# State recurrence of an S5 layer: a third chain on GpSimd, and conditioning loads issued by the sync engine

## What is computed

```
bu = einsum('blgh,gph->blgp', u, bb)             # input to the states
s_t = a * s_(t-1) + bu_t                         # complex, diagonal; scan over the positions
y = einsum('blgp,ghp->blgh', s_re, c_re) - einsum('blgp,ghp->blgh', s_im, c_im)
z = gelu(d*u + y_forward + y_backward) @ w_glu
```

## Time and profile before

| | us |
|---|---|
| median of 3 runs | 3016.66 |
| lowest and highest run | 3013.38, 3018.93 |
| the profiled execution | 3012.23 |
| its span from first to last instruction | 3010.4 |
| recurrence on VectorE, first to last start | 1856.9 to 1948.4 |
| its 124 products, 128 x 256 elements, mean | 0.412 |
| its 248 sums, 128 x 128 elements, mean | 0.279 |

### The profile page before, as it was taken

The page is one execution under the profiler, slowest core; times in us unless marked ns, Lnnn a source line. Parts: engine busy times, 40 slices in busy tenths (PEclk is TensorE's granted clock), DMA queues, the critical chain, the costliest instruction groups (busy, mean ns, idle before and its releaser), DMA issues.

```text
span 3010.4 us, 42044 instructions
## 1 busy us (share of the span) xinstructions
PE 2663.3 (88%) x16522; PEld 2155.4 (72%) x16522; DVE 1925.7 (64%) x1959; ACT 1073.1 (36%) x856; POOL 112.0 (4%) x169
## 2 busy tenths in 40 slices
PE   6969999986368899999999985759979999999997
PEld 3438888722357788888888873258868888888886
DVE  7866666544955677676777763846676666655554
ACT  3333333323313333333443423023433333344442
POOL 1020000000000100000000002110001000000000
PEclk9989999988678999999999997979989999999999
DMA  8988888544004388787887859667837777555551
GB/s 246 351 275 269 277 268 275 170 127 152 0 0 154 113 279 279 258 285 267 281 276 261 284 175 210 182 172 258 289 134 235 234 241 235 192 193 185 181 182 55
DMA packets 289270, 639.64 MB, mean 212 GB/s; under 512 B 76371, under 2 KB 79317, under 8 KB 285589
## 3 DMA queue, kind: packets, MB, share of 16 engines
q1 hardware_dynamic: 243844, 601.22, 60.6%
q0 software_dynamic: 6400, 19.21, 2.2%
q10 hardware_dynamic: 38928, 17.86, 2.2%
HBM read 614.24 MB, written 19.79 MB: 211 GB/s over the span
## 4 chain that ended last, share of the span: by engine, by line
PE 76%; DVE 12%; DMA 4%; ACT 3%; ACTq 3%; issue 2%; SPq 1%; DVEq 0%
PE PS L267 45%; PE PS L268 23%; DMA araw<-in_ada_w 2%; ACTq L972 2%; ACT Pb L928 2%; DVE Pb L1639 2%; DVE acc L1634 1%; PE PS L873 1%; PE PS L449 1%; PE PS L714 1%; PE PS L220 1%; PE PS L735 1%; PE PS L184 1%; DMA omat<-WF 1%; DVE HF L1567 1%
## 5 line engine op out<-in xcount | busy, mean ns | idle before, releaser
L267 PE MATMUL PS<-H,whi 128*128 128x512 f32 x5888 | 2077.8, 398 | 98.7 <-DVE wlo L257 75.3
L268 PE MATMUL PS<-H,wlo 128*128 128x256 f32 x5888 | 1653.3, 281 | 0.0
L267 PEld LDWEIGHTS PS<-H,whi 128*128 128x128 f32 x5888 | 1112.9, 189 | 366.7 <-DVE wlo L257 81.4
L257 DVE TENSOR_TENSOR wlo<-raw,whi 128x2048 fp32r<-128x2048 f32 x368 | 843.1, 2292 | 734.0 <-ACT whi L253 733.1
L253 ACT ACTIVATE whi<-raw 128x2048 fp32r<-128x2048 f32 x368 | 705.5, 1918 | 1252.9 <-PE PS L268 1219.4
L268 PEld LDWEIGHTS PS<-H,wlo 128*128 128x128 f32 x5888 | 1118.7, 190 | 0.0
L176 DVE SCALAR_TENSOR_TENSOR acc<-araw,cact,acc 128x1024 f32<-128x1024 f32 x240 | 307.0, 1279 | 0.7 <-DMA araw<-in_ada_w 0.3
L928 ACT ACTIVATE Pb<-PS 128x1024 f32 (+5 forms) x117 | 118.3, 1035 | 180.9 <-issue 69.3
L928 ACT ACTIVATE H<-Pb 128x512 fp32r (+2 forms) x142 | 94.9, 669 | 42.2 <-DVE Pb L1338 28.3
L1745 POOL TENSOR_SCALAR X<-X,small 128x256 f32<-128x256 f32 x64 | 54.7, 867 | 1084.0 <-DVE Pb L1338 1083.9
L1386 DVE TENSOR_TENSOR H<-Pb,H 128x512 fp32r<-128x512 f32 x128 | 87.5, 684 | 0.0
(11 more groups left out here) (251 smaller groups left out, 1446.6 us busy)
## 6 DMA issues: line engine op xcount, KB each, us to landing
raw<-in_mlp_w SPq DMA_DIRECT2D x256, 1024.0 KB, 6.1
araw<-in_ada_w SPq DMA_DIRECT2D x308, 512.0 KB, 4.4
raw<-in_mix_w_in SPq DMA_DIRECT2D x64, 1024.0 KB, 7.7
raw<-in_s_w_glu SPq DMA_DIRECT2D x32, 1024.0 KB, 7.4
acc<-in_ada_w SPq DMA_DIRECT2D x44, 512.0 KB, 6.9
raw<-in_mix_w_out SPq DMA_DIRECT2D x16, 1024.0 KB, 5.1
vmat<-Pb ACTq DMA_DIRECT2D x8, 1024.0 KB, 7.6
omat<-WF ACTq DMA_DIRECT2D x16, 512.0 KB, 13.2
```

What stands on the lines that cost most here:

```text
L257: nc.vector.tensor_tensor(wlo[:, s % 2, :], raw[:, s, :], whi[:, s % 2, :].bitcast(F), ALU.subtract).then_inc(S("lo_done"), 1)
L267: nc.tensor.matmul(PS[:, b, :], w[0], H2[:, :, k, :], start=first, stop=False, skip_group_check=True)
L268: return nc.tensor.matmul(PS[:, b, 0:T], w[1], H2[:, 0, k, :], start=False, stop=last, skip_group_check=True)
```

## The change

VectorE keeps 96 of the 128 groups, as two chains of 48 with a semaphore each. The other 32 groups go to GpSimd as a third chain, with its own semaphore and its own products in `acc[:, 512:640]`. The instructions are the same on both engines and are written once, in `recurrence`. GpSimd starts its chain when all increments are copied and the first state is zeroed. TensorE waits for both engines before `across`. The 32 loads of the shift parts leave GpSimd's queue, and SP issues them, with the same waits, between the inner matrices and the last four output matrices.

```diff
-    STP = acc[:, 0:512].rearrange("p (h a c x) -> p h a c x", h=2, a=2, c=2)
+    STP = acc[:, 0:384].rearrange("p (h a c x) -> p h a c x", h=2, a=2, c=2)
+    STP_POOL = acc[:, 512:640].rearrange("p (h a c x) -> p h a c x", h=1, a=2, c=2)
+
+    def recurrence(engine, q, chains, products):
+        A4v = A4[:].rearrange("p (a c) x -> p a c x", a=2)
+        done = 0
+        for k in range(2, 64):
+            for h, (steps, xs) in enumerate(chains):
+                if k > 2:
+                    q.wait_ge(S(steps), done)
+                old = SV[:, k - 1, :, xs].unsqueeze(1).broadcast_to([P, 2, 2, xs.stop - xs.start])
+                engine.tensor_tensor(products[:, h], A4v[:, :, :, xs], old, ALU.mult).then_inc(S(steps), 1)
+            for a_ in range(2):
+                for h, (steps, xs) in enumerate(chains):
+                    q.wait_ge(S(steps), done + 1 + a_)
+                    new = SV[:, k, :, xs]
+                    engine.tensor_tensor(new, new, products[:, h, 1, ::-1] if a_ else products[:, h, 0], ALU.add
+                                         ).then_inc(S(steps), 1)
+            done += 3
+        for steps, _ in chains:
+            q.wait_ge(S(steps), done)
...
@@ sync, after the loads of IM
+                    sp.wait_ge(S(f"{GATE2.name}_freed"), 1)
+                    for c in range(32):
+                        if c < 4:
+                            sp.wait_ge(S("ada_used"), SCALE3.base + PRIME_ADA)
+                        else:
+                            sp.wait_ge(S("shift_used"), c - 3)
+                        row, col = (3 * KT + c // 2) * P, (c % 2) * ADA_HALF
+                        sp.dma_start(SHB[c % 4], ada_w[row:row + P, col:col + ADA_HALF]
+                                     ).then_inc(S(f"sh_ready{c % 4}"), 16)
...
@@ tensor
-                pe.wait_ge(S("s5_scan"), 1)
+                pe.wait_ge(S("s5_scan"), 2)
...
@@ vector: the loop over k with its two halves is replaced by
+                    recurrence(nc.vector, v, (("scan_steps", slice(0, 48)), ("scan_other", slice(48, 96))), STP)
                     v.sem_inc(S("s5_scan"), 1)
...
@@ gpsimd: the loop of 32 loads is replaced by
+            pool.wait_ge(S("sv_evac"), 8)
+            pool.wait_ge(S("win_ready"), 3)
+            recurrence(nc.gpsimd, pool, (("pool_steps", slice(96, 128)),), STP_POOL)
+            pool.sem_inc(S("s5_scan"), 1)
```

## The result

Over 20 runs of each, the changed kernel has a median of 3022.8 us against 3010.73 us: ratio 1.0034, with a 95% interval of 1.0018 to 1.0050, some 5 to 15 us. The forecast was slower, by 68 us.

What follows compares the result with a forecast made beforehand. VectorE's recurrence in layer 1 was taken to set the end, TensorE waiting 9.6 us. VectorE's 75 us plus GpSimd's 85 us against 91.9 gave +68 us on 3012.2, 3080, set at 3082 us; range 3015 to 3105.

Steps and rivals of the forecast that it cites:

- The sign: Whole kernel: the change makes it slower, by 68 us in the likeliest case; chance of slower 0.81.
- the order, one chain after the other: Layer 1's recurrence: GpSimd stands still until VectorE's chains end, so 75 + 85 = 160 us against 91.9; chance 0.53.
- The rival by turns: Recurrence: GpSimd gets in after each VectorE instruction, costing VectorE 0.52 us a step; +15 to +30 us, 3027 to 3047; chance 0.27.
- VectorE alone: Recurrence: VectorE's 96 groups need 1.21 us a step, 75.1 us for 62 steps.
- GpSimd alone: Recurrence: GpSimd's product and two sums need 1.37 us a step, 85 us in all, bounds 74 and 91.
- Serial order: Recurrence: VectorE's chains, then GpSimd's, take 160 us together, from 1856.9 to 2017.
- The clock behind the scan: TensorE after the recurrence: a longer wait costs next to nothing more in clock, 27 products a us against 28.
- The loads: Conditioning loads moved to SP: first lands near 1885, TensorE ready at 1948 to 1956, hidden behind the scan; uncovered -1 to +7 us.
- The 9.6 us as the most to be had: TensorE's wait before line 873: the most a shorter recurrence can give with everything else left alone.

Runs made afterwards that it cites:

- the experiment on kinds: Changed kernel with GpSimd's chain replaced by chained MEMSETs, TENSOR_SCALARs, COPYs and sums, 32 of 128 groups not computed; the first TENSOR_SCALAR took 51.8 us, VectorE ended at 1942.9.

## Why the prediction was wrong

**The sign was right, the size was not**, and it was one step: "I read from that that VectorE keeps GpSimd out until its own chains are done". The rows behind it are true. They show TENSOR_SCALARs with their scalars in SBUF, and such an instruction is kept out of the recurrence for 51 us in the experiment on kinds. The chain of the change is made of TENSOR_TENSORs. These enter at every boundary of VectorE's long instructions, and between the short ones with a mean delay of 0.03 us. So the term of the sum that failed is the order, one chain after the other, 75 + 85 = 160 us: measured are 107.1 us, of which GpSimd runs beside VectorE for 88.2. The recurrence grew by 15 us and not by 68. The trace before had the warning in it: a COPY got in at 40.61. I explained this by the gap of 0.033 us in front of VectorE's next instruction, when the kind of GpSimd's instruction had changed as well. More than one thing differed between the earlier trace rows, and I gave the effect to one.

**The rival by turns** was the case: VectorE loses 31.8 us / 62 = 0.51 us for each step of GpSimd, where it had said 0.52, and needs 107.1 us, where it had said 107. That this agrees to the hundredth is in part luck: its 1 ns a value came from one TENSOR_SCALAR with scalars in SBUF, a kind that enters otherwise and costs 0.8 ns a value (0.20 us for 256), and the kinds measured since cost 0.7 to 1.0. Its other half was off. It let GpSimd wait 0.1 to 0.2 us an instruction, and GpSimd lost 6 us in 186 instructions, 0.03 each. Its time, 3027 and more, lies above the measured median of 3022.8; on the footing of the 20 runs of before, 3010.73, its +15 lies at the upper end of the interval.

**The Trainium skill**, "SBUF — State Buffer", "Who interferes with whom", says that a VectorE instruction with two SBUF inputs contends with a GpSimd instruction that reads SBUF, not with one that only writes it. The traces agree: VectorE's step grew from 1.21 to 1.57 us and more beside instructions that read, MEMSETs had no effect, and with one of VectorE's inputs in PSUM neither had the reads. The Trainium skill's rule, in "Summary: rules for kernel authors" of the same page, that the second to issue blocks until the first has finished, holds for GpSimd's sums, 1.18 us beside VectorE's long instructions, which start 1.26 us apart. It doesn't hold for a TENSOR_SCALAR with scalars in SBUF, which waited through some 250 of VectorE's instructions. And where VectorE is the second, it loses less than the length of GpSimd's instruction: 0.12 us for a sum that lasts 0.32.

**VectorE alone**: 75.1 us predicted, 75.3 measured with GpSimd silent. **GpSimd alone**: 85 predicted, 82.0 measured, inside the bounds of 74 and 91. Here errors cancelled: a product takes 0.45 us and a sum 0.32, less than taken from the rows (a COPY of 128 takes 0.30 when undisturbed, not the 0.41 of the earlier trace rows), but the hand-over to the next instruction takes 0.078, not 0.033. **Serial order**: 160 predicted, 157.4 measured, in the kernel that enforces it. These terms were right; what failed was putting one after the other. **The clock behind the scan** cost nothing more: after the wait of 14.1 us the first 6.2 us ran at a mean granted 0.62 with 172 products, against 0.82 and 171 in the same stretch of before.

**The loads**: small rows done near 1882 and the first part near 1885 predicted, 28 us after the start of the recurrence; TensorE began at 1884.51, 30.6 us after a start that came 3 us earlier in that run. TensorE ready 91 to 99 us after the start predicted, 93.05 measured. The conclusion held too: the loads alone take the whole room of 9.6 us, at no cost of their own that can be told from the noise (0.9993).

**The 9.6 us as the most to be had** held for the program as it stood, as the prediction had said ("with everything else left alone"), and is no limit of the idea: with the small rows moved away TensorE was ready 66.8 us after VectorE's first product.

## What to carry to other kernels

GpSimd beside VectorE is no free engine: when VectorE's instructions have two inputs in SBUF and GpSimd's read SBUF, count for each GpSimd instruction what it takes from VectorE (0.17 us here), and look first whether one operand of VectorE's can live in PSUM, which took the whole cost away here. When two engines' overlap is read off rows, match the kind of instruction and its operands on both sides, not only engine and size. And before shortening one of two parallel chains, ask when the other is done, above all if the change moves its loads behind thousands of small rows on one queue.

## What the hardware showed that was not expected

- A GpSimd TENSOR_SCALAR of 256 elements with its scalars in SBUF takes 0.55 us undisturbed. The one that stood beside the recurrence took 51.8 us, those beside sums of 128 took 0.91 us (four of VectorE's instructions), and those beside sums of 1024 3.5 to 3.6 us (three). The same instruction with constants takes 0.43 us beside the recurrence.
- GpSimd's chain of TENSOR_TENSORs is hardly slowed by VectorE (82.0 to 88.2 us), VectorE is by 42% (75.3 to 107.1 us), and by 56% while both work (a step of 1.89 us against 1.21).
- VectorE's instructions of 96 and 192 elements are as fast with one input in PSUM as with both in SBUF: 73.7 us against 75.3 for the same 372.
